# Weighting expert rows in place and summing them by accumulating transposes

## What is computed

```python
def block(args):
    hb, eb, gb = args
    act = jax.nn.gelu(jnp.einsum('tkd,td->tk', u[eb], hb), approximate=False)
    return jnp.einsum('tk,tkd->td', (gb * act).astype(hb.dtype), v[eb])
```

## Time and profile before

| | |
|---|---|
| median of three runs | 3835.97 us (3833.49 to 3836.34) |
| profiled execution, first to last instruction | 3833.0 us |
| instructions | 37262 |
| TensorE busy | 3320.4 us (87%) |
| VectorE busy | 2747.0 us (72%) |
| ScalarE busy | 1637.5 us (43%) |
| GpSimd busy | 1505.8 us (39%) |
| HBM traffic | 1460.36 MB, mean 381 GB/s |
| mean granted TensorE clock | 0.975 |

### The profile page before, as it was taken

How to read it: one execution, slowest core, us unless ns; L and a number is a source line. 1 busy time by engine, 2 the same in 40 slices (tenths; PEclk the granted TensorE clock), 3 DMA queues, 4 the chain that set the end, 5 groups by cost and what they waited for, 6 DMA issues and landing times. The chain is left out here.

```text
span 3833.0 us, 37262 instructions
## 1 busy us (share of the span) xinstructions
PE 3320.4 (87%) x9664; PEld 1675.5 (44%) x9664; DVE 2747.0 (72%) x6373; ACT 1637.5 (43%) x4800; POOL 1505.8 (39%) x1323
## 2 busy tenths in 40 slices
PE   8988888888988988999999888888788888888887
PEld 4443433334444444455555456644333333433332
DVE  5867767767989888566665567677877767767765
ACT  3134444444555544443333325534444444444443
POOL 0034444434444444444444410044444444444442
PEclk9999999999999999999999998999999999999999
DMA  8389999999999999999999982099999999999997
GB/s 313 134 358 419 419 420 409 420 420 402 412 399 419 388 420 419 397 419 419 420 417 420 419 332 88 11 408 418 420 420 411 420 418 417 404 420 417 414 413 330
DMA packets 202918, 1460.36 MB, mean 381 GB/s; under 512 B 23120, under 2 KB 23504, under 8 KB 27600
## 3 DMA queue, kind: packets, MB, share of 16 engines
q0 software_dynamic: 189936, 1377.91, 87.5%
q1 hardware_dynamic: 12768, 80.07, 5.3%
HBM read 1455.79 MB, written 2.10 MB: 380 GB/s over the span
## 5 line engine op out<-in xcount | busy, mean ns | idle before, releaser
L1617 PE MATMUL ps<-arena 128*128 128x512 f32 x4888 | 2334.5, 616 | 444.1 <-ACT arena L1665 440.4
L1795 POOL DMA_INDIRECT arena<-experts,arena x1280 | 1484.1, 1159 | 2057.1 <-PE ps L1617 1607.2
L1698 DVE CUSTOM_DVE_ANT_0 arena<-arena 128x1024 f32<-128x1024 f32 x1280 | 1557.0, 1224 | 757.2 <-DMA arena<-experts,arena 738.8
L1617 PEld LDWEIGHTS ps<-arena 128*128 128x128 f32 x4888 | 891.2, 193 | 1695.4 <-ACT arena L1665 870.8
L1654 ACT ACTIVATE arena<-arena 128x1 f32<-128x1 f32 x1280 | 258.1, 202 | 1579.7 <-DVE arena L1698 1569.0
L1665 ACT ACTIVATE arena<-arena 128x128 f32<-128x128 f32 x1222 | 490.7, 402 | 89.7 <-issue 4.4
L1658 ACT ACTIVATE arena<-arena 128x1 f32<-128x1 f32 x1280 | 377.0, 295 | 90.4 <-issue 3.1
L1327 PE MATMUL ps<-arena 128*128 128x256 f32 x1280 | 289.5, 379 | 1.1 <-ACT arena L1479 1.1
L1327 PEld LDWEIGHTS ps<-arena 128*128 128x128 f32 x1280 | 241.8, 190 | 60.6 <-issue 30.3
L713 PE MATMUL ps<-arena 128*128 128x256 f32 x1024 | 235.7, 384 | 7.3 <-PEq L1801 7.3
L713 PEld LDWEIGHTS ps<-arena 128*128 128x128 f32 x1024 | 198.1, 194 | 62.3 <-issue 37.7
(11 more groups left out here) (185 smaller groups left out, 2089.9 us busy)
## 6 DMA issues: line engine op xcount, KB each, us to landing
arena<-experts,arena POOLq DMA_INDIRECT x1280
arena<-diff_w_in SPq DMA_DIRECT2D x20, 1024.0 KB, 7.6
arena<-w_mod SPq DMA_DIRECT2D x16, 1024.0 KB, 5.0
arena<-w_late POOLq DMA_DIRECT2D x16, 1024.0 KB, 5.6
arena<-peer_wq SPq DMA_DIRECT2D x12, 1024.0 KB, 12.0
arena<-w_mod SPq DMA_DIRECT2D x4, 2048.0 KB, 18.0
arena<-w_early SPq DMA_DIRECT2D x8, 1024.0 KB, 9.1
arena<-b_mod POOLq DMA_DIRECT2D x12, 512.0 KB, 9.2
```

What stands on the lines that cost most here:

```text
L1617: last = nc.tensor.matmul(acc(t)[:, half * 512:(half + 1) * 512], diag[:, placed(n) % DIAGS, :], ring[:, slot_of(n), D + half * 512:D + (h ...
L1698: nc.vector.tensor_tensor_reduce(out=u_row, in0=u_row, in1=h_of(t), scale=1.0, scalar=0.0, op0=ALU.mult, op1=ALU.add, accum_out=dots[:, j: ...
L1795: nc.gpsimd.indirect_dma_start(out=ring[:, slot_of(n), :], out_offset=None, in_=experts, in_offset=bass.IndirectOffsetOnAxis(ap=idx_sb[:, ...
```

## The change

VectorE now weights expert rows 2, 7 and 12 of every unit, and ScalarE the other thirteen, both in place in the ring slot, over all 1024 columns of v. No diagonal is made any more. TensorE accumulates the transposes of the weighted row's eight 128x128 blocks in PSUM, so that `acc` holds the transposed sum. When a tile is done, ScalarE copies it to SBUF (`sums_out`), TensorE turns it back with eight more transposes (`sums_back`, in the next tile's first unit after expert row 6), and `finish_tile` waits for that. VectorE's own sum and `add_row` are gone. The semaphores that count once or more per unit are shared by the layers, which changes their names and values alone.

```diff
-        def added(n):
-            u, j = n // TOPK, n % TOPK
-            if layer == 0:
-                return u > SIDE + 2 and j in ((4, 8, 13) if u % PEER_HEADS else (13,))
-            return u < 6 and j in (4, 8, 13)
+        VECTOR_ROWS = (2, 7, 12)
+        def by_vector(n):
+            return n % TOPK in VECTOR_ROWS
+        def scale_row(dve, n):
+            W(dve, "weights", by_vector_before(n) + 1)
+            row, j = ring[:, slot_of(n), D:2 * D], n % TOPK
+            nc.vector.tensor_scalar(row, row, act_out[:, j:j + 1], None, ALU.mult).then_inc(S("scaled_vector"), 1)
...
+        def sums_out(act, t):
+            W(act, "acc", 2 * t + 1)
+            nc.scalar.copy(h_of(t), acc(t)).then_inc(S("sums_out"), 1)
+        def sums_back(pe, t):
+            W(pe, "sums_out", t + 1)
+            for k in range(KD):
+                last = nc.tensor.transpose(acc(t)[:, k * P:(k + 1) * P], h_of(t)[:, k * P:(k + 1) * P], pid)
+            last.then_inc(S("acc"), 1)
...
         def finish_tile(dve, t):
-            W(dve, "acc", t + 1)
-            if ADDED[(t + 1) * PEER_HEADS * TOPK] > ADDED[t * PEER_HEADS * TOPK]:
-                nc.vector.tensor_tensor(sum_of(t), sum_of(t), acc(t), ALU.add).then_inc(S("acc_free"), 1)
-                dve.drain()
-                nc.vector.tensor_tensor(h_of(t), sum_of(t), mod_of(t, 2), ALU.mult)
-            else:
-                nc.vector.tensor_tensor(h_of(t), acc(t), mod_of(t, 2), ALU.mult).then_inc(S("acc_free"), 1)
+            W(dve, "acc", 2 * t + 2)
+            nc.vector.tensor_tensor(h_of(t), acc(t), mod_of(t, 2), ALU.mult).then_inc(S("acc_free"), 1)
...
 pe_unit:
-                if not added(n):
-                    W(pe, "diag", placed(n) + 1)
-                    for half in range(2):
-                        last = nc.tensor.matmul(acc(t)[:, half * 512:(half + 1) * 512], diag[:, placed(n) % DIAGS, :],
-                                                ring[:, slot_of(n), D + half * 512:D + (half + 1) * 512],
...
+                if by_vector(n):
+                    W(pe, "scaled_vector", by_vector_before(n) + 1)
+                else:
+                    W(pe, "scaled", n + 1 - by_vector_before(n))
+                row = ring[:, slot_of(n), D:2 * D]
+                for k in range(KD):
+                    last = nc.tensor.matmul(acc(t)[:, k * P:(k + 1) * P], row[:, k * P:(k + 1) * P], pid,
+                                            is_transpose=True, start=(head == 0 and j == 0 and k % 4 == 0),
+                                            stop=(head == PEER_HEADS - 1 and j == TOPK - 1), skip_group_check=True)
+                last.then_inc(S("slots_free"), 1)
+                if t and head == 0 and j == 6:
+                    sums_back(pe, t - 1)
...
 act_unit:
-                    nc.scalar.activation(diag[:, placed(n) % DIAGS, :], pid, ACT.Copy, scale=act_out[:, j:j + 1]
-                                         ).then_inc(S("diag"), 1)
+                    row = ring[:, slot_of(n), D:2 * D]
+                    nc.scalar.activation(row, row, ACT.Copy, scale=act_out[:, j:j + 1]).then_inc(S("scaled"), 1)
+                if u // PEER_HEADS and u % PEER_HEADS == 0 and b == 1:
+                    sums_out(act, u // PEER_HEADS - 1)
...
 dve_unit, after the dot product of expert row n:
-                    if j >= 2 and added(n - 2):
-                        add_row(dve, n - 2)
+                    if j >= 2 and by_vector(n - 2):
+                        scale_row(dve, n - 2)
```

More of the change, by code:

```diff
@@ L34 @@
 AHEAD_UNITS = 20
-DIAGS = 4
 SINGLE = 16
@@ L91 @@
 A_YTMP_AT = 13312
-SUM_AT = (7168, 5120)
 HCUR_AT = 12288
@@ L96 @@
 PHT_AT = 14336
-DIAG_AT = 15360
 IDX_AT = 15872
@@ L1206, in peer, with S, W @@
         n_ = f"e{layer}_"
-        S = lambda name: sem(n_ + name)
-        W = lambda eng, name, value: wait(eng, n_ + name, value)
+        PER_UNIT = {"dots": TOPK, "slots_free": TOPK, "idx": 1, "gates": 1, "expo": 1, "best": 1, "weights": 3, "scaled_vector": 3, "scaled": TOPK - 3}
+        def S(name):
+            return sem("e_" + name if name in PER_UNIT else n_ + name)
+        def W(eng, name, value):
+            if name in PER_UNIT and value > 0:
+                wait(eng, "e_" + name, layer * NT * PEER_HEADS * PER_UNIT[name] + value)
+            elif name not in PER_UNIT:
+                wait(eng, n_ + name, value)
         tiles = len(order)
@@ L1267, in peer, with by_vector_before @@
         OUT_HALVES = {(0, 3): (1, 0), (0, 11): (1, 1), (1, 6): (2, 0), (1, 14): (2, 1), (2, 8): (3, 0), (2, 15): (3, 1)}
-        def added(n):
-            u, j = n // TOPK, n % TOPK
-            if layer == 0:
-                return u > SIDE + 2 and j in ((4, 8, 13) if u % PEER_HEADS else (13,))
-            return u < 6 and j in (4, 8, 13)
[L1276 to L1286, removed]
-        def slot_free(pool, n):
[L1289 to L1300, removed]
-            else:
-                last = nc.vector.scalar_tensor_tensor(out=a, in0=row, scalar=act_out[:, j:j + 1], in1=a,
-                                                      op0=ALU.mult, op1=ALU.add)
-            last.then_inc(S("rows_added"), 1)
-            dve.drain()
+        VECTOR_ROWS = (2, 7, 12)
+        def by_vector(n):
+            return n % TOPK in VECTOR_ROWS
+        def by_vector_before(n):
+            return n // TOPK * len(VECTOR_ROWS) + sum(1 for j in VECTOR_ROWS if j < n % TOPK)
+        def scale_row(dve, n):
+            W(dve, "weights", by_vector_before(n) + 1)
+            row, j = ring[:, slot_of(n), D:2 * D], n % TOPK
+            nc.vector.tensor_scalar(row, row, act_out[:, j:j + 1], None, ALU.mult).then_inc(S("scaled_vector"), 1)
+        def slot_free(pool, n):
+            W(pool, "slots_free", n + 1)
         def paired(r):
@@ L1613, in pe_unit @@
                 n = u * TOPK + j
-                if not added(n):
-                    W(pe, "diag", placed(n) + 1)
-                    for half in range(2):
-                        last = nc.tensor.matmul(acc(t)[:, half * 512:(half + 1) * 512], diag[:, placed(n) % DIAGS, :],
-                                                ring[:, slot_of(n), D + half * 512:D + (half + 1) * 512],
-                                                start=(head == 0 and j == 0),
-                                                stop=(head == PEER_HEADS - 1 and j == TOPK - 1), skip_group_check=True)
-                    last.then_inc(S("slots_free"), 1)
+                if by_vector(n):
[10 more added lines that the diff above has]
+                    sums_back(pe, t - 1)
                 if r and j == 1:
@@ L1659, in act_unit @@
                                                   scale=gate_sb[:, u % AHEAD_UNITS, j:j + 1])
-                    if added(n):
+                    if by_vector(n):
                         weight.then_inc(S("weights"), 1)
@@ L1663, in act_unit @@
                     act.drain()
-                    W(act, "slots_free", placed(n) - DIAGS + 1)
-                    nc.scalar.activation(diag[:, placed(n) % DIAGS, :], pid, ACT.Copy, scale=act_out[:, j:j + 1]
-                                         ).then_inc(S("diag"), 1)
+                    row = ring[:, slot_of(n), D:2 * D]
+                    nc.scalar.activation(row, row, ACT.Copy, scale=act_out[:, j:j + 1]).then_inc(S("scaled"), 1)
+                if u // PEER_HEADS and u % PEER_HEADS == 0 and b == 1:
+                    sums_out(act, u // PEER_HEADS - 1)
                 if r and b == (2 if len(r) == 1 else 1):
@@ L1860, in _ @@
                         pe_unit(pe, u)
+                    sums_back(pe, tiles - 1)
                 @block.scalar
@@ L1873, in _ @@
                         act_unit(act, u)
+                    sums_out(act, tiles - 1)
                 @block.vector
```

3 lines of the change are left out of this document (removed).

## The result

The change makes the kernel slower by half a per cent: 3855.86 us, the median of four runs (3852.63 to 3858.91), against 3835.17 us for the kernel before on the same chip. The ratio is 1.0056, with a 95% interval of 1.0044 to 1.0068. The forecast was 3851 us.

What follows compares the result with a forecast made beforehand. Transfers were taken to bound most units, VectorE nearly bounding units 17 to 26. Terms 13.2 + 1 + 1.6 + 0.4 - 1 gave +15 us on 3836, so 3851 us, range 3830 to 3874.

Steps and rivals of the forecast that it cites:

- The 960 us less of TensorE work: Whole kernel: transposes at 0.94 us a row replace products at 1.77; worth nothing beside transfers that last as long.
- around the span as 3 us: Whole kernel: the median time of 3836.0 us stood 3 us above the profiled span of 3833.0.
- VectorE in units 17 to 26: Two-head units: 30 added scales, 22.5 us, less 9.3 us absorbed by waits for landings; +13.2 us, bounds +7.5 and +22.5.
- The new wait behind late rows: TensorE waits for rows 2, 7, 12 that VectorE scales late, delaying rows and products behind; nothing, at worst 5 us.
- Unit 33: ScalarE's side-work unit gains 7 us of work, inside its waits on average; +1 us, between 0 and 4.
- TensorE's relief: At 200 to 240 and 1580 to 1620 us, missing bandwidth partly regained; -1 us, between 0 and 8 gained.
- The end: After the last row: longer scale, shorter row, then copy of the sum and eight transposes; +1.6 us.
- Rival A: Whole kernel faster: TensorE keeps slots from coming free and its relief refills the queue; 3824 us, chance 0.13.
- Rival B: Units 17 to 26: TensorE's lateness goes and hides VectorE's addition, costing 0 to 5 us; 3839 us, chance 0.22.
- Rival C: TensorE idles more, so its granted clock drops to perhaps 0.7; 10 to 40 us, middle 3876, chance 0.11.
- Its far end: Transposes alone never bring the clock back: 325 us more, 4176 us; chance 0.04 together with the unoverlapped transposes.
- 45 us of transposes that don't overlap: Two-head units: at 0.273 us per transpose TensorE would bound them, 45 us in all; 0.04 shared with the clock's far end.

Runs made afterwards that it cites:

- none, one, three and five rows: Expert rows VectorE scales per unit in units 17 to 26, against the kernel before: whole-kernel ratios 1.0013, 1.0026, 1.0056 and 1.0086.
- dead work: All sixteen expert rows by ScalarE, plus five unread 128x512 VectorE tensor_scalar per unit in units 17 to 26; 3848.36 us, 1.0041 of the kernel before.
- with the rows moved: Changed kernel with VectorE's rows at 3, 8, 13 instead of 2, 7, 12 in units 16 to 31 and from 34 on; 3853.84 us.
- with the rows moved away: Changed kernel with VectorE's rows at 3, 8, 13 from unit 34 on in layer 0 (1.0046), or also in units 16 to 31 (1.0059).
- all-ScalarE kernel: Changed kernel with all sixteen expert rows of every unit weighted by ScalarE, none by VectorE; 3837.9 us, 1.0013 of the kernel before.
- all-ScalarE kernel with products: All expert rows weighted by ScalarE, added by products with the identity instead of the changed kernel's transposes; 3871.95 us, 1.0099 of the kernel before.
- five-row kernel: Changed kernel with VectorE weighting rows 2, 4, 7, 9, 12 in units 17 to 26, 2, 7, 12 elsewhere; 3863.5 us, 1.0086 of the kernel before.

## Why the prediction was right

The reading of what bounds held, and the largest term, VectorE's added work in units 17 to 26, is real. That 3851 came within 5 us is in part luck. The profiled spans differ by 20.9 us. Units 17 to 26, unit 33 and the end, for which the forecast had 15.8, gave 12.8; the other 8 net come from stages that it had at next to nothing. The 960 us less of TensorE work by the forecast's account (678 by the page's busy time, over the whole kernel) bought nothing in the plain units, because transfers pay for them. That account took 0.94 us per row of transposes; at the granted clock they took 1594.2 us of busy time, 1.25 us a row:

```profile
L1613 PE MATMUL ps<-arena 128*128 128x128 f32 x10240 | 1594.2, 321 | 1141.3 <-DVE arena L1288 699.0
```

What the forecast put around the span as 3 us is 1.8 us in the runs (3855.69 us for a span of 3853.9); the sum doesn't depend on it. Point by point:

- **VectorE in units 17 to 26**: forecast +13.2, measured +10.0. The mechanism is right: none, one, three and five rows give -0.2, +1.3, +10.0 and +21.8 us, and dead work lengthens the stage too, by 7.7 us. Both terms were mis-sized. The scales cost 18.2 us of VectorE's time and not 22.5, because I charged durations and not distances; and the waits they went into were 9.4 us, of landings and of the exponential together, where the sum took the 9.3 of landings alone. I had the second wait as a bound only.
- **The new wait behind late rows**: forecast 0, at worst 5. In the two-head units that is what it was: with the rows moved, the stage was the same within 1 us. In units 34 to 46 it made waits that the forecast didn't have. Before, a projection product followed a row that ScalarE had weighted; now the fourth one follows row 12, which VectorE scales after the dot product of row 14, and VectorE then waits for that product itself. The waits in units 34 to 45, kernel after:

```profile
DVE arena L747 <- PE ps L710: 37.0, 9, 5.6
DVE arena L736 <- PE ps L710: 15.1, 4, 5.4
```

Before, the same two waits were 3.8 and 1.0 us. The 52 us lie mostly beside transfers: VectorE's waits for landings fell from 167.5 to 142.0 us there, and the stage grew by 4.8 us or, cut one unit earlier, by 0.3. No run shows that this cost anything in the whole kernel: with the rows moved away the times are 1.0046 and 1.0059, with them 1.0056. I had costed the side stage at nothing by its DMA share and had followed the late row only through the two-head units.

- **Unit 33**: forecast +1, measured +0.2. **TensorE's relief**: forecast -1; the share at 200 to 240 us went from 0.71 to 0.74, 11 GB/s or 1 us, and the window at 1590 to 1630 us is full now, at 420 GB/s. But that stretch of units did not get shorter.
- **The end**: forecast +1.6, measured +2.6. The end of the kernel after, from the timeline (start us, us, engine):

```profile
3836.40 5.20 PE L1613 MATMUL ps<-arena 128*128 128x128 f32 x32 [5.23 <-DVE arena L1288]
...
3838.83 1.15 ACT L1662 ACTIVATE arena<-arena 128x1024 f32<-128x1024 f32 x1
...
3841.68 1.01 ACT L1547 COPY arena<-ps 128x1024 f32<-128x1024 f32 x1 [1.70 <-PEq L1640]
...
3842.74 0.86 PEld L1553 LDWEIGHTS ps<-arena 128*128 128x128 f32 x8 [1.39 <-ACT arena L1547]
...
3843.88 1.23 DVE L1559 TENSOR_TENSOR arena<-ps,arena 128x1024 f32<-128x1024 f32 x1 [5.71 <-PE ps L1553]
```

The copy and the turning back take 1.01 and 1.09 us, as forecast. The last scale takes 1.15, and here the earlier rows are late: TensorE's work on rows 12 to 15 is one piece of 32 transposes that begins only when VectorE has scaled row 12, 5.2 us after TensorE last had anything. That this makes the extra microsecond is not shown: the three kernels in which VectorE has no row at the end and the sum is turned back have ends 3.7 to 4.8 us longer than before.
- **Rival A** (faster, by refilled queues) failed: the all-ScalarE kernel gives TensorE all its relief and VectorE no work, and units 17 to 26 are no shorter than before (ScalarE's added work is in it too; these runs don't show what the relief would give without that). **Rival B** (VectorE's work hidden, 0 to 5 us) failed: it cost 10 us. **Rival C** (the clock): the clock did fall, to 0.848 overall and 0.80 to 0.84 in the plain and two-head units, less far than the 0.7 forecast. Its price was put at 10 to 40 us; 0.831 comes with 1.0013 (1.0004 to 1.0022), 4 us for everything in that kernel, so the clock's own price doesn't stand out. Its far end, transposes that never bring the clock back, is excluded by the last section's rows, and so are the 45 us of transposes that don't overlap.

What I did not foresee is what the all-ScalarE kernel with products showed: the relief that I wrote off as worth nothing is needed, once ScalarE takes 1.8 us per row, to keep that kernel from being 1% slower. The transposes pay for the scale in place; none of these kernels gets more than that out of them.

The +3.7 us in layer 1 before the last unit have no experiment of their own and their cause stays open. Four kernels with the same layer 1 have +2.7 to +3.8 there, but the five-row kernel, whose layer 1 is also the same, has -0.4; those without VectorE's rows have -0.3 to +2.7. In units 54 to 78 there are 0.6 to 2.9 us in every kernel here that scales in place, with VectorE's rows or without.

## What to carry to other kernels

Before moving work from the busiest engine, find in windows by stage which resource sets each stage, and give the moved work to an engine that has room in the tightest stage, not on average: VectorE was busy for 72% overall and for 90% where it counted. The wait time that an engine has in that stage is roughly what it can take for nothing, and in this kernel each microsecond after that cost one; count the added work by the distance between neighbouring starts, not by durations. A step that is handed to an in-order engine's queue two items later delays everything behind it in its consumer, so look at what the consumer issues directly after that item. Here that made some 50 us of waits, most of them beside transfers that paid for the stage anyway.

## What was unexpected of the hardware

The clock came back under transposes alone. Stretches of the kernel after, cut where the granted clock changes, in a plain unit (share of full clock in the column before DMA share):

```profile
470.50:473.80 3.30, 0.78 (x4) 0.35 (x2) 2.29 (x6) 1.52 (x3) 0.15 (x1) 1.00 1.00 410
474.00:477.20 3.20, 3.16 (x15) 3.16 (x16) 2.31 (x6) 2.36 (x4) 0.92 (x1) 0.50 1.00 415
477.40:480.50 3.10, 2.17 (x20) 1.93 (x18) 2.03 (x3) 2.99 (x6) 2.32 (x2) 1.00 1.02 423
480.80:484.10 3.30, 1.09 (x8) 0.86 (x8) 2.83 (x8) 2.30 (x7) 0.95 (x2) 1.00 1.01 420
484.30:491.00 6.70, 4.49 (x21) 4.49 (x22) 4.67 (x9) 5.06 (x10) 1.65 (x2) 0.50 1.01 418
```

At 470.5 to 473.8 us TensorE ends a query product and falls idle, and the granted clock drops to 1.2 GHz. In 474.0 to 477.2 it does nothing but expert-row transposes, 15 on record in 3.2 us and so 0.21 us each, and from 477.4 on it has 2.4 GHz again, where eight take 1.09. It then does one expert row of eight transposes, idles, and from 484.3 on is at half clock again. The Trainium skill (TensorE: Matmul & The Clock Gate, Part 4) says that full clock does not engage for transposes and that they do not count as busy in the same way; for these float32 transposes this trace disagrees. The some 275 ns that the page gives for one transpose of bf16 in a kernel is near the duration seen here for float32 (273), but not the price of one in a stream (eight in 1.09 us).

An in-place activation over 128x1024 floats took 1.149 us (1.147 to 1.158 over 1040 of them), against 1.048 for the squares of the same width that are the nearest rows before. No run here tells which difference between the two makes that tenth.
